# Choosing experts inside the experts' stage, beside memory products and first tiles, and moving the third layer's memory products to the delta rule

## The chip, the cores and the metric

The kernel runs as one program on one core of a Trainium2 chip. The metric is the device time of one execution, in microseconds (us). The data are float32. Matrix products of fp32r tiles are made from a leading and a trailing part of each number, so that a weight is first split on two engines and then multiplied.

## The reference

256 tokens of width 2048 pass one layer of a first model, then two layers of a second. The first layer mixes (short convolution and a state space), attends to a memory of 256 rows, and ends with 16384 experts. Each of the two layers after it uses a memory of its own model, the same for both.

In short, with eight heads and 128 keys a side (the 16384 experts are the pairs of keys):

```
def first_block(x, mem, ...):
    h = h + concat(rms_norm(conv), rms_norm(s5)) @ w_out
    h = h + mem_cross_attention(rms_norm(h), rms_norm(mem), ...)
    h = h + peer(rms_norm(h), w_q, sub_keys, u_tab, v_tab)
    return rms_norm(h, final_norm_g)

def peer(h, w_q, sub_keys, u_tab, v_tab):
    q = (h @ w_q).reshape(..., PEER_HEADS, 2, PEER_HALF)
    s = einsum("blhsk,hsnk->blhsn", q, sub_keys)
    s1, i1 = top_k(s[..., 0, :], 16); s2, i2 = top_k(s[..., 1, :], 16)
    top_s, pos = top_k(s1[:, None] + s2[None, :], 16)
    idx = i1 * 128 + i2 at pos;  g = softmax(top_s)
    act = gelu(h . u_tab[idx]);  return sum(g * act * v_tab[idx])
```

```
def memory_attention(q, gate, mem, mem_gain, w_kv, q_gain, k_gain):
    mk, mv = split_cols(rms_norm(mem, mem_gain) @ w_kv, [512, 512])
    ...
def gdn_branch(...):    
    q, k = l2_norm(q), l2_norm(k)
    o = gated_delta_chunked(...) forward + the same backward
    return rms_norm(o, out_gain) * silu(gate)
```

`gdn_branch` is in the second layer. The memory's keys and values (`mk`, `mv`) depend on the input alone, so they can be computed at any time before the layer that reads them. There are four such products of 2048 x 512: key and value of the second layer (k2, v2) and of the third (k3, v3).

## The kernel before

The program is a row of stages. A stage owns its buffers and semaphores, runs one block of code for each engine, and ends with a barrier of all engines. When a certain number of semaphores is spent (`MOST_SEMS`), they are cleared between two stages.

Weights come as pieces of 512 KB into a ring of four slots (`WeightRing`), loaded by SyncE in the order of the table `JOBS`, four pieces ahead of their use. A piece is split: ScalarE writes its leading part (L415, in the experts L2509), VectorE subtracts to get the trailing part (L420, in the experts L2593), and TensorE multiplies (L548, L2439). Two halves of a linear are thus worked on by three engines in step. The memory products are an exception: they multiply the piece unsplit (`rest_raw`, L2116).

**The load stage** (`load_inputs`) sends small tables, all of x in one transfer of 2 MB, the first constants and four weight pieces from SyncE, and waits for the first three.

**The experts** are three stages (`experts`). The first is the query's linear. The second, "topk" (`choose_experts`), computes scores on TensorE, and VectorE finds the sixteen best of each head (maxima, their indices, replacement; then the sums; then a decoding of places into two indices by comparison, multiplication and reduction, L2276 to L2291). Beside it `MemoryBeside` makes the four memory products in eight turns on TensorE, with one accumulator of two banks, each product evicted by ScalarE (L2126, L2133) before the next starts; SyncE stores the four results to DRAM. The last softmax step (Exp, L2195) stands behind these evictions on ScalarE. The third stage, "dense" (`dense_experts`), multiplies all 16384 experts. Its up half has 32 tiles of eight pieces. A tile's results lie in banks 0 to 3; ScalarE takes the low half out, VectorE adds the rest (L2601, which frees the banks) and scales it, ScalarE applies the gelu, and GpSimd spills the result to DRAM. During the first sixteen tiles TensorE also lays out the gates of the chosen experts as small one-hot products (L2419) in banks 4 to 7, from tables that VectorE weighs (L2614, L2617); for that the choices are first transposed on TensorE (L2475) and copied by VectorE (L2654). GpSimd stores the gates, and at tile 16 fetches two pieces of 2 MB back with four small ones. The down half has 64 steps, which use all eight banks.

**The delta rule** is in the second layer (`even_layer`): `delta_prepare` (transposes L3062, sums of squares as one-column matmuls L1550, spreading of the norms L1582), then the items, then `head_norm` (sums L800, rows L815) and `gate_by_silu`, two stages, and then the output's linear (L548).

## Time and profile before

| what | value |
|---|---|
| three runs | 4055.44, 4059.89, 4064.39 us |
| median | 4059.89 us |
| profiled execution | 4056.16 us |
| its span | 4054.4 us |
| mean granted TensorE clock | 0.97 of full speed |
| TensorE busy | 3849.8 us (95%) |
| VectorE busy | 2435.8 us (60%) |
| ScalarE busy | 1629.8 us (40%) |
| GpSimd busy | 143.4 us (4%) |

A "hole" below is a stretch in which TensorE has no matmul. A row of a timeline gives the start, the length, the engine, the line and the instruction, how many of them in a row, and in brackets the idle time before it and what ended it. PEq is TensorE's own sequencer. Of the 1.8 us between span and execution nothing is seen. The row of granted clock in the page is in tenths of full speed (2.4 GHz); half of it is the lower level, 1.2 GHz.

### The profile page before, as it was taken

What the parts mean: (1) busy time and instruction counts of PE and PEld (TensorE: products, weight loads), DVE (VectorE), ACT (ScalarE), POOL (GpSimd) and SP (SyncE); (2) the same over time, 40 slices, a digit from 0 to 9 for tenths busy, and PEclk for the clock granted to TensorE, in tenths of its full rate; (3) what the DMA queues carried; (4) which work ended last, traced back from release to release, by engine and by line L of the source; (5) the groups of instructions that cost most, each with busy time, mean ns of one, the idle gap of its engine ahead of it and who ended that gap; (6) DMA issues with size and microseconds to landing.
All of it is one profiled execution on the core that took longest, in us unless ns stands there. A gap on an engine that the chain in (4) does not pass through costs nothing. (4 is left out here: it accounts for less than half of the span.)

```text
span 4054.4 us, 66104 instructions
## 1 busy us (share of the span) xinstructions
PE 3849.8 (95%) x25800; PEld 3428.8 (85%) x25800; DVE 2435.8 (60%) x3651; ACT 1629.8 (40%) x2127; POOL 143.4 (4%) x228
## 2 busy tenths in 40 slices
PE   8989899989899999999999999899999889998999
PEld 8975599987688888888888888798999879898989
DVE  5679755459577764556656555544595654565454
ACT  4214344341244444444444444433344333443443
POOL 0002000000000000000000000000000000000000
PEclk9999999999999999999999999899998989998999
DMA  6544355443566676667777776466343015543345
GB/s 221 155 145 140 95 167 167 125 151 111 185 224 222 216 237 231 202 207 240 242 236 238 240 236 206 133 184 206 94 130 110 2 35 174 164 135 125 116 125 166
DMA packets 189107, 682.88 MB, mean 168 GB/s; under 512 B 26568, under 2 KB 29128, under 8 KB 186704
## 3 DMA queue, kind: packets, MB, share of 16 engines
q1 hardware_dynamic: 172624, 608.84, 48.8%
q0 software_dynamic: 16096, 70.26, 4.6%
q8 instruction: 167, 2.74, 0.3%
q10 hardware_dynamic: 160, 0.54, 0.0%
q14 instruction: 60, 0.49, 0.0%
HBM read 639.70 MB, written 39.86 MB: 168 GB/s over the span
## 5 line engine op out<-in xcount | busy, mean ns | idle before, releaser
L2593 DVE TENSOR_TENSOR dense_weights_trailing<-weight_ring,dense_weights_leading 128x1024 fp32r<-128x1024 f32 x512 | 627.2, 1225 | 562.9 <-ACT dense_weights_leading L2509 562.5
L2509 ACT ACTIVATE dense_weights_leading<-weight_ring 128x1024 fp32r<-128x1024 f32 x512 | 542.4, 1060 | 768.7 <-PE dense_banks L2439 368.1
L420 DVE TENSOR_TENSOR held_trailing<-weight_ring,held_leading 128x1024 fp32r<-128x1024 f32 x440 | 537.2, 1226 | 489.1 <-ACT held_leading L415 486.4
L415 ACT ACTIVATE held_leading<-weight_ring 128x1024 fp32r<-128x1024 f32 x440 | 464.6, 1058 | 781.9 <-PE lin_in_acc L548 247.8
L2439 PE MATMUL dense_banks<-pe_parts,dense_weights_leading 128*128 128x512 f32 x2048 | 735.8, 404 | 10.9 <-DVE dense_act_in L2601 9.0
L2468 PE MATMUL dense_banks<-dense_weights_leading,dense_act_parts 128*128 128x512 f32 x2048 | 630.5, 389 | 0.0
L2439 PE MATMUL dense_banks<-pe_parts,dense_weights_trailing 128*128 128x256 f32 x2048 | 554.0, 281 | 0.0
L2439 PEld LDWEIGHTS dense_banks<-pe_parts,dense_weights_leading 128*128 128x128 f32 x2048 | 380.0, 189 | 93.5 <-DVE dense_weights_trailing L2593 9.5
L2468 PEld LDWEIGHTS dense_banks<-dense_weights_leading,dense_act_parts 128*128 128x128 f32 x2048 | 384.4, 188 | 79.8
L2468 PE MATMUL dense_banks<-dense_weights_trailing,dense_act_parts 128*128 128x512 f32 x1024 | 398.3, 389 | 0.0
L2439 PEld LDWEIGHTS dense_banks<-pe_parts,dense_weights_trailing 128*128 128x128 f32 x2048 | 388.5, 190 | 10.0
L548 PE MATMUL lin_out_acc<-lin_out_parts,held_leading 128*128 128x256 f32 x1280 | 233.7, 286 | 15.3 <-DVE held_trailing L420 9.5
L2468 PEld LDWEIGHTS dense_banks<-dense_weights_trailing,dense_act_parts 128*128 128x128 f32 x1024 | 192.2, 188 | 39.9
L548 PEld LDWEIGHTS lin_out_acc<-lin_out_parts,held_leading 128*128 128x128 f32 x1280 | 202.3, 194 | 15.6 <-issue 15.6
L548 PE MATMUL lin_in_acc<-od_parts,held_leading 128*128 128x256 f32 x1024 | 199.8, 296 | 3.2 <-DVE od_parts L660 3.2
L548 PE MATMUL lin_att_acc<-ev_parts,held_leading 128*128 128x256 f32 x1024 | 188.5, 287 | 14.5 <-DVE held_trailing L420 14.5
L548 PE MATMUL lin_in_acc<-ev_parts,held_leading 128*128 128x256 f32 x1024 | 195.4, 292 | 2.0 <-DVEq L646 2.0
L548 PE MATMUL lin_out_acc<-lin_out_parts,held_trailing 128*128 128x256 f32 x640 | 182.5, 285 | 0.0
L548 PEld LDWEIGHTS lin_att_acc<-ev_parts,held_leading 128*128 128x128 f32 x1024 | 162.0, 194 | 16.2 <-issue 15.7
L548 PEld LDWEIGHTS lin_in_acc<-od_parts,held_leading 128*128 128x128 f32 x1024 | 166.8, 198 | 5.9 <-issue 3.4
L548 PEld LDWEIGHTS lin_in_acc<-ev_parts,held_leading 128*128 128x128 f32 x1024 | 163.6, 195 | 4.8 <-DVEq L646 2.4
L548 PE MATMUL lin_in_acc<-lin_in_parts,lin_in_weights_leading 128*128 128x256 f32 x768 | 143.7, 289 | 14.4 <-DVE lin_in_weights_trailing L420 14.4
(735 smaller groups left out, 6871.4 us busy)
## 6 DMA issues: line engine op xcount, KB each, us to landing
weight_ring<-in_w_up SPq DMA_DIRECT2D x256, 512.0 KB, 4.2
weight_ring<-in_w_down SPq DMA_DIRECT2D x256, 512.0 KB, 4.3
weight_ring<-in_w_in SPq DMA_DIRECT2D x176, 512.0 KB, 3.7
weight_ring<-in_w_out SPq DMA_DIRECT2D x112, 512.0 KB, 4.0
weight_ring<-in_w_att SPq DMA_DIRECT2D x64, 512.0 KB, 3.6
weight_ring<-in_w_gate SPq DMA_DIRECT2D x40, 512.0 KB, 3.6
weight_ring<-in_w_key SPq DMA_DIRECT2D x32, 512.0 KB, 3.5
weight_ring<-in_w_value SPq DMA_DIRECT2D x32, 512.0 KB, 3.6
```

The costliest lines, as they stand in the source:

```text
L415: self.nc.scalar.activation(leading, x, ACT.Copy).then_inc(self.led, 1)
L420: return self.nc.vector.tensor_tensor(trailing, x, leading.bitcast(F32), ALU.subtract)
L548: mm = nc.tensor.matmul(acc[:, half, sub], still, moving, start=begin and m == 0, stop=end and m == 2, skip_group_check=not tokens)
L2439: mm = nc.tensor.matmul(to, still, moving, start=begin and m == 0, stop=end and m == 1)
L2468: mm = nc.tensor.matmul(banks[:, down_at[n] + t], still, moving, start=begins and j == 0 and m == 0, stop=ends and j == blocks - 1 and m == 2)
L2509: nc.scalar.activation(ring.leading[:, b], ring.ring[:, b], ACT.Copy).then_inc(split_led, 1)
L2593: v.tensor_tensor(ring.trailing[:, b], ring.ring[:, b], ring.leading[:, b].bitcast(F32), ALU.subtract).then_inc(ring.split, 1)
```

## The change

The change has six parts.

1. The stage "topk" goes away. `dense_experts` starts with scores and the memory products of the second layer (k2, v2); each has two banks of its own. VectorE's work is cut into 110 turns (a generator, `ChooseExperts.on_vector`): 62 before the first tile, then one after each weight piece of tiles 0 to 7 but the third of each, behind which the add of the tile before stands. Pieces are split as before.
2. The gates are laid out in tiles 8 to 23 (`lay_from`, `lay_to`) instead of 0 to 15. From tile 24 odd tiles use banks 4 to 7. GpSimd fetches the first gate piece at tile 24 and the second at tile 28 (`stagger`). ScalarE's Exp stands at the 45th piece of the tiles.
3. To have room, x is kept in DRAM during the experts (`x_kept`, two stores with the fetches of the query's linear, fetched back at the start of the down half); its place holds squares and results of the memory products.
4. k3 is made in `delta_prepare`, v3 in the new `close_delta`, which also takes the place of `head_norm` and `gate_by_silu`. ScalarE multiplies the memory by the layer's gain in the first; GpSimd stores the result for the second, and k3; `close_delta` stores v3 from ScalarE. The table of jobs follows.
5. The load stage sends x in four parts, each followed by a weight piece, and the first linear waits for each part (`src_here`); the stage waits for the small tables alone.
6. `MOST_SEMS` is 72 instead of 60. By the order of the stages semaphores are now cleared at five stage ends instead of three.

```diff
 JOBS = [
-    ("peer_q", 2, 8), ("memk2", 1, 8), ("memv2", 1, 8), ("memk3", 1, 8), ("memv3", 1, 8), ("up", 32, 8), ("down", 32, 8),
-    ("att2", 8, 8), ("dv2", 2, 8), ("in2", 8, 8), ("out2", 4, 10), ("in3", 8, 8), ("upk", 2, 2), ("upv", 2, 2),
+    ("peer_q", 2, 8), ("memk2", 1, 8), ("memv2", 1, 8), ("up", 32, 8), ("down", 32, 8),
+    ("att2", 8, 8), ("dv2", 2, 8), ("in2", 8, 8), ("memk3", 1, 8), ("memv3", 1, 8), ("out2", 4, 10), ("in3", 8, 8), ("upk", 2, 2), ("upv", 2, 2),
...
-    MOST_SEMS = 60
+    MOST_SEMS = 72
...
                 sp.dma_start(k.cols[:], a["cols"]).then_inc(here, 16)
-                sp.dma_start(k.x[:], a["x_t"]).then_inc(here, 16)
+                part(0)
+                ring.load(sp, 0, 0)
                 sp.dma_start(k.consts[:, 0:FIRST_CONSTS], a["consts"][:, 0:FIRST_CONSTS]).then_inc(here, 16)
-                ring.start(sp, 0)
-                sp.wait_ge(here, 48)
+                for n in range(1, X_PARTS):
+                    part(n)
+                    ring.load(sp, 0, n)
+                sp.wait_ge(here, 32)
...
+    lay_from, lay_to, exp_piece, stagger = 8, 24, 44, 4
...
+        def up_banks(i, m):
+            return 4 if from_tile(i, m, lay_to) and m % 2 else 0
...
+                    if t == lay_to:
+                        for b in range(2):
+                            pool.wait_ge(stored[b], 16 * ((lay_to - lay_from) // 2))
+                        fetch_gate(0)
...
+                    if t == lay_to + stagger:
+                        fetch_gate(1)
...
+                for turn in range(memory.JOBS * memory.HALVES):
...
+                    memory.on_tensor(pe, turn)
+                for m in range(lay_from):
+                    up_tile(0, m, False, False)
+                pe.wait_ge(choice.picked, 1)
+                pe.wait_ge(memory.evicted, 2)
...
+                        if c == 2 and not at_tile(i, m, 0):
+                            add(i, m - 1)
+                        if choosing and (c != 2 or m == 0):
+                            next(turns, None)
...
+                for _ in range(choice.EARLY):
+                    next(turns, None)
+                for m in range(lay_from):
+                    up_tile(0, m, False, True)
+                for _ in turns:
+                    pass
                 for n, x in enumerate((first_t, second_t, weight_t)):
                     dve.wait_ge(flipped, n + 1)
...
+            def _(pool):
+                for q in range(4):
+                    pool.wait_ge(featured[q], 16)
+                    pool.dma_start(k.memory_feats[:, quarter(q)], feats[:, quarter(q)]).then_inc(kept, 16)
+                pool.wait_ge(keyed, 1)
+                pool.dma_start(k.memory[2], key[:].rearrange("p a t -> p (a t)")).then_inc(kept, 16)
+                pool.wait_ge(kept, 80)
...
                     norms.sum(pe, 2 * m + 1)
-                for g in order:
+                memory.on_tensor(pe, 0)
+                memory.on_tensor(pe, 1)
+                for at, g in enumerate(order):
                     norms.spread_out(pe, g)
...
+                    if at % 2 == 0 and at < 6:
+                        memory.on_tensor(pe, 2 + at // 2)
+                for c in range(5, 8):
+                    memory.on_tensor(pe, c)
...
                 for g in range(8):
                     norms.square(act, g)
+                    if g >= 4:
+                        q = g - 4
+                        act.wait_ge(mem_here[q], 16)
+                        for c in range(4 * q, 4 * q + 4):
+                            nc.scalar.activation(feats[:, c], feats[:, c], ACT.Copy,
+                                                 scale=k.col("od_mem_norm")[:, c:c + 1]).then_inc(featured[q], 4)
...
+def close_delta(k, ring, y, gate, gain, x_back):
...
+            @block.tensor
+            def _(pe):
+                memory.on_tensor(pe, 0)
+                for c in range(chunks):
+                    if c % 2 == 0:
+                        pe.wait_ge(squared, c // 2 + 1)
...
+                mm.then_inc(summed, 1)
+                memory.on_tensor(pe, 1)
+                pe.wait_ge(inverted, 1)
...
+                for c in range(2, 8):
+                    memory.on_tensor(pe, c)
...
-        head_norm(k, y[:, 0:8], 8, 1, P, k.col("ev_gdn_norm"), here=x_back)
-        gate_by_silu(k, y[:, 0:8], proj[:, 24:32], 8)
+        close_delta(k, ring, y[:, 0:8], proj[:, 24:32], k.col("ev_gdn_norm"), x_back)
```

TensorE at the start of the experts' tiles, before. `one_h` and `pe_mem` are the memory times the gain of the second and of the third layer:

```order
L2205 MATMUL topk_score<-topk_keys,pe_query 128x128 x4
L2116 MATMUL topk_mem_acc<-one_h,weight_ring 128x256 x64
L2116 MATMUL topk_mem_acc<-weight_ring,one_h 128x512 x32
L2116 MATMUL topk_mem_acc<-pe_mem,weight_ring 128x256 x64
L2116 MATMUL topk_mem_acc<-weight_ring,pe_mem 128x512 x32
L2168 UNCONDITIONAL_BRANCH
L2408 UNCONDITIONAL_BRANCH
L2475 MATMUL dense_banks<-consts,pe_first 128x128 x2
L2475 MATMUL dense_banks<-consts,pe_second 128x128 x2
L2475 MATMUL dense_banks<-consts,pe_weight 128x128 x2
L2439 MATMUL dense_banks<-pe_parts,dense_weights_leading 128x512
```

The same place after:

```order
L2182 MATMUL dense_banks<-dense_low,pe_query 128x128 x4
L2117 MATMUL dense_banks<-one_h,weight_ring 128x256 x64
L2117 MATMUL dense_banks<-weight_ring,one_h 128x512 x32
L2453 MATMUL dense_banks<-pe_parts,dense_weights_leading 128x512
L2453 MATMUL dense_banks<-pe_parts,dense_weights_trailing 128x256
```

Two products, the end of a stage and the six transposes no longer stand between the scores and the first tile; the transposes (now L2505) stand behind tile 7.

VectorE where the choices are copied, before, at the head of the first tile:

```order
L2654 COPY dense_first_t<-dense_banks 128x256
L2654 COPY dense_second_t<-dense_banks 128x256
L2654 COPY dense_weight_t<-dense_banks 128x256
L2593 TENSOR_TENSOR dense_weights_trailing<-weight_ring,dense_weights_leading 128x1024
L2614 TENSOR_SCALAR dense_weighed<-consts,dense_second_t,dense_weight_t 128x128 x2
```

After, in tile 8:

```order
L2720 COPY dense_first_t<-dense_banks 128x256
L2720 COPY dense_second_t<-dense_banks 128x256
L2720 COPY dense_weight_t<-dense_banks 128x256
L2641 TENSOR_TENSOR dense_weights_trailing<-weight_ring,dense_weights_leading 128x1024
L2664 TENSOR_SCALAR dense_laying<-consts,dense_second_t,dense_weight_t 128x128 x2
L2641 TENSOR_TENSOR dense_weights_trailing<-weight_ring,dense_weights_leading 128x1024
L2664 TENSOR_SCALAR dense_laying<-consts,dense_second_t,dense_weight_t 128x128 x2
L2641 TENSOR_TENSOR dense_weights_trailing<-weight_ring,dense_weights_leading 128x1024
L2664 TENSOR_SCALAR dense_laying<-consts,dense_second_t,dense_weight_t 128x128 x2
L2650 TENSOR_TENSOR dense_act_in<-dense_low,dense_banks 128x512 x2
```

The add of tile 7 (the last row), which frees its banks, now stands behind three copies, three splits and three weighings; in the first tile there was no earlier tile to add.

TensorE in the preparation of the delta rule, after, from the last sums of squares on. Before, the rows of L1595 (then L1582) stood in one line of x20 behind the sums, and there was no L3121:

```order
L1563 MATMUL prepare_sums<-consts,prepare_sq 128x1 x8
L3121 MATMUL prepare_mem_acc<-prepare_mem_feats,weight_ring 128x256 x16
L1595 MATMUL prepare_rows<-consts,prepare_heads_scale 128x128 x4
L3121 MATMUL prepare_mem_acc<-prepare_mem_feats,weight_ring 128x256 x8
L1595 MATMUL prepare_rows<-consts,prepare_heads_scale 128x128 x8
L3121 MATMUL prepare_mem_acc<-prepare_mem_feats,weight_ring 128x256 x8
...
L3179 MATMUL prepare_turned<-consts,ev_proj 128x128 x4
L3121 MATMUL prepare_mem_acc<-prepare_mem_feats,weight_ring 128x256 x24
```

The first two pieces of the product come between the sums and the rows, three between the rows, and three behind all else.

## Rows read from the trace of the kernel before

**Rows 1.** The page: busy time of the engines; VectorE's splits (line, operation, count, busy, mean).

```profile
PE 3849.8 (95%) x25800; PEld 3428.8 (85%) x25800; DVE 2435.8 (60%) x3651; ACT 1629.8 (40%) x2127; POOL 143.4 (4%) x228
...
L2593 DVE TENSOR_TENSOR dense_weights_trailing<-weight_ring,dense_weights_leading 128x1024 fp32r<-128x1024 f32 x512 | 627.2, 1225 | 562.9 <-ACT dense_weights_leading L2509 562.5
...
L2439 PE MATMUL dense_banks<-pe_parts,dense_weights_leading 128*128 128x512 f32 x2048 | 735.8, 404 | 10.9 <-DVE dense_act_in L2601 9.0
```

**Rows 2.** TensorE's waits: who waited for whom, total us, times, longest.

```profile
PE lin_att_acc L548 <- DVE held_trailing L420: 14.5, 1, 14.5
...
PE dense_banks L2439 <- DVE dense_act_in L2601: 9.0, 15, 5.7
```

**Rows 3.** Groups by line, 900 to 1080 us: busy us, mean ns, idle before.

```profile
L2116 PE MATMUL topk_mem_acc<-one_h,weight_ring 128*128 128x256 f32 x128 | 29.0, 390 | 0.0
...
L2116 PE MATMUL topk_mem_acc<-pe_mem,weight_ring 128*128 128x256 f32 x128 | 27.9, 380 | 1.4 <-ACT mem_v L2133 1.4
...
L2116 PE MATMUL topk_mem_acc<-weight_ring,pe_mem 128*128 128x512 f32 x64 | 27.7, 593 | 1.2 <-ACT mem_k L2126 1.2
```

**Rows 4.** Timeline of VectorE, choosing: last reduce of the first decode; the wait for Exp.

```profile
966.14 2.33 DVE L2291 TENSOR_REDUCE pe_second<-topk_hit_b 128x64 f32<-128x1024 f32 x2
...
1050.42 0.42 DVE L2307 TENSOR_REDUCE topk_total<-topk_raw 128x16 f32<-128x256 f32 x1 [30.26 <-ACT topk_raw L2195]
```

**Rows 5.** Timeline, from the first product to the third weighing of the first tile.

```profile
931.18 28.97 PE L2116 MATMUL topk_mem_acc<-one_h,weight_ring 128*128 128x256 f32 x128
...
1059.86 0.66 PE L2475 MATMUL dense_banks<-consts,pe_first 128*128 128x128 f32 x2 [12.57 <-PEq L2168]
...
1063.26 0.80 PE L2439 MATMUL dense_banks<-pe_parts,dense_weights_leading 128*128 128x512 f32 x1 [1.89 <-DVE dense_weights_trailing L2593]
...
1066.42 0.60 DVE L2614 TENSOR_SCALAR dense_weighed<-consts,dense_second_t,dense_weight_t 128x128 f32<-128x128 f32 x2
```

**Rows 6.** Timeline of TensorE, one-column sums before and in the delta preparation, and its end.

```profile
3066.66 1.84 PE L1550 MATMUL lin_in_beside<-consts,lin_in_biased 128*128 128x1 f32 x16
...
3119.81 3.41 PE L1550 MATMUL prepare_sums<-consts,prepare_sq 128*128 128x1 f32 x16
...
3125.04 6.36 PE L1582 MATMUL prepare_rows<-consts,prepare_heads_scale 128*128 128x128 f32 x40 [1.82 <-DVE prepare_heads_scale L365]
...
3137.52 1.04 PE L3296 MATMUL delta_big<-gd_decay,consts 128*128 128x8 f32 x8 [1.58 <-PEq L3048]
```

**Rows 7.** Timeline of TensorE from the items' end to the output's linear.

```profile
3305.79 6.98 PE L800 MATMUL hnorm_sums<-consts,hnorm_sq 128*128 128x1 f32 x32 [2.30 <-ACT hnorm_sq L789]
...
3314.47 6.13 PE L815 MATMUL hnorm_row<-consts,hnorm_scale 128*128 128x128 f32 x32 [1.70 <-DVE hnorm_scale L365]
...
3330.15 0.77 PE L548 MATMUL lin_out_acc<-lin_out_parts,held_leading 128*128 128x256 f32 x2 [9.55 <-DVE held_trailing L420]
```

**Rows 8.** Windows: stretch, length, busy PE PEld DVE ACT POOL (count), clock, DMA, GB/s.

```profile
1600.00:1650.00 50.00, 49.57 (x279) 42.27 (x277) 26.68 (x27) 22.90 (x26) 1.07 (x2) 1.00 0.64 208
1533.00:1536.00 3.00, 3.00 (x11) 2.52 (x11) 2.37 (x4) 0.04 (x1) 0.00 (x0) 0.50 0.77 303
3107.00:3125.00 18.00, 16.18 (x80) 15.86 (x78) 4.58 (x13) 7.43 (x11) 0.00 (x0) 0.52 0.42 145
```

**Rows 9.** Groups by line, 1250 to 1300 us: VectorE's add of a tile's halves.

```profile
L2601 DVE TENSOR_TENSOR dense_act_in<-dense_low,dense_banks 128x512 f32<-128x512 f32 x4 | 2.7, 684 | 0.9 <-ACT dense_low L2517 0.9
```

**Rows 10.** Timeline of ScalarE, after the gate fetches.

```profile
1525.08 1.06 ACT L2509 ACTIVATE dense_weights_leading<-weight_ring 128x1024 fp32r<-128x1024 f32 x1 [5.45 <-DMA weight_ring<-in_w_up]
```

**Rows 11.** Timeline of the first linear: first matmul; the split that waited for a weight piece.

```profile
14.42 0.77 PE L548 MATMUL lin_in_acc<-lin_in_parts,lin_in_weights_leading 128*128 128x256 f32 x2 [14.42 <-DVE lin_in_weights_trailing L420]
...
23.90 1.06 ACT L415 ACTIVATE lin_in_weights_leading<-weight_ring 128x1024 fp32r<-128x1024 f32 x1 [2.76 <-DMA weight_ring<-in_w_in]
```

**Rows 12.** DMA issues: transfers, KB each, us from issue to landing.

```profile
memory_rows<-mem_v SPq DMA_DIRECT2D x2, 512.0 KB, 4.2
```

More of the change, by code:

```diff
@@ L295, in __init__ @@
         self.x = sb("x", [P, DC, SEQ])
+        self.x_here = [stack.enter_context(nc.semaphore(f"x_here{n}")) for n in range(X_PARTS)]
     def const(self, name):
@@ L2315, in dense_experts, with key_on_scalar, value_on_scalar @@
-def dense_experts(k, ring, parts, scale, first, second, weight, gates, acts, spare):
-    nc = k.nc
-    job = ring.at
-    ring.at += 2
+    def key_on_scalar(self, act):
+        act.wait_ge(self.ring.freed, self.first + 8)
+        self.k.nc.scalar.activation(self.outs[0].rearrange("p (a b) t -> p a (b t)", a=2), self.acc[0],
+                                    ACT.Copy).then_inc(self.evicted, 1)
+    def value_on_scalar(self, act):
+        act.wait_ge(self.ring.freed, self.first + 16)
+        act.wait_ge(self.col_made, 1)
+        value = self.outs[1].rearrange("p (t a) f -> p t (a f)", t=TILES)
+        for t in range(TILES):
+            ins = self.k.nc.scalar.activation(value[:, t], self.acc[1][:, t], ACT.Copy, scale=self.col[:, t:t + 1])
+        ins.then_inc(self.evicted, 1)
@@ L2323, in dense_experts @@
+def dense_experts(k, ring, parts, scale, query, first, second, weight, gates, acts, mem, here, x_kept):
+    nc = k.nc
     groups, per, blocks, slots = 8, 32, ring.BLOCKS, ring.SLOTS
-    assert ring.jobs[job][2:] == ring.jobs[job + 1][2:] == (32, 8)
-    up_base, down_base = ring.first[job], ring.first[job + 1]
-    side, laying_groups, tiles, steps, ahead = 8, 4, 32, 64, 2
-    laying_tiles = 4 * laying_groups
+    side, tiles, steps, ahead = 8, 32, 64, 2
+    lay_from, lay_to, exp_piece, stagger = 8, 24, 44, 4
@@ new lines, in dense_experts @@
+        choice = ChooseExperts(k, s, query, low[:].rearrange("p a b (c f) -> p (a b c) f", f=PEER_KEYS), laying, staging, banks,
+                               first, second, weight, memory)
+        with ExitStack() as early:
+            choice.on_early_memory(lambda n, shape, dt=F32: early.enter_context(nc.sbuf_tensor(f"{s.name}_{n}", shape, dt)))
+        act_parts = s.sb("act_parts", [P, 4, 2, 2, SEQ], F32R)
+        job = ring.at
+        ring.at += 2
+        assert ring.jobs[job][2:] == ring.jobs[job + 1][2:] == (32, 8)
@@ L2437, in up_tile @@
                                 pairs = (rest, high) if end else (high, rest)
-                                for m, (still, moving, to) in enumerate(pairs):
-                                    mm = nc.tensor.matmul(to, still, moving, start=begin and m == 0, stop=end and m == 1)
+                                for n, (still, moving, to) in enumerate(pairs):
+                                    mm = nc.tensor.matmul(to, still, moving, start=begin and n == 0, stop=end and n == 1)
                             if c == 7 and sub == 1:
@@ L3511, in _, with delta_rule @@
                     pass
-def delta_rule(k, proj, ba, spare, out, back):
+def delta_rule(k, ring, proj, ba, spare, out, back):
     nc = k.nc
```

807 lines of the change are left out of this document (467 added, 340 removed).

## The prediction

> **What bounds the kernel now.** I read the page's engine shares first: TensorE is busy 3849.8 us of a 4054.4 us span, VectorE only 60% [rows 1]. So time comes off only where TensorE stops, where it runs at the lower clock, or where its work goes away. I then read TensorE's waits: no total is over 15 us, and the two rows taken here are the largest and the one of the experts' tiles [rows 2]. The idle time lies in some thirty small holes, mostly at stage ends. Last I read the three places that the diff touches.
>
> The experts' start: TensorE does four memory products one after the other, keys 29.0 and 27.9 us, values 27.7 each, with waits of 1.2 to 1.4 us between them [rows 3], while VectorE chooses experts. VectorE is not the bound: after its last reduce at 1020.2 it waits 30.3 us for ScalarE's Exp, which stands behind the last eviction of those products [rows 4]. Then come the end of the stage, 12.6 us of idle TensorE, six transposes, and the first tile's matmul at 1063.26 [rows 5]. The two halves of the third layer's work (about 56 us) delay the experts although nobody there needs them.
>
> The delta preparation: TensorE is the bound, at 1.2 GHz. Sixteen one-column matmuls take 3.41 us there and 1.84 us where the clock is full. There is little idle: 1.8 us before the spreading of the norms into rows, 1.6 us at the end [rows 6]. Closing the delta rule: 26.7 us from the first stop to the output projection's first matmul, with idle pieces of 2.3, 1.7 and 9.55 us and the rest at the low clock (32 one-column matmuls in 6.98 us, 0.22 each, against 1.84/16 = 0.115) [rows 6, 7].
>
> So the change moves 56 us of TensorE work from one place where TensorE is the bound to two where it is almost so. My sum is made against the profiled run's own 4056.16 us; the median of before is 3.7 us above that.
>
> **The change part by part.**
>
> *Start of the tiles.* The products begin at 931.18 [rows 5], as now. Two remain: 29.0 + 27.7, without the 1.2 us wait for an eviction, since they have their own banks. TensorE is at the first tile at 987.9 instead of 1063.26: **-75.4**. After the hole the tile's first matmuls run at the low level (0.80 us for the first [rows 5], 404 ns in the mean [rows 1]), for about 3.2 us by my count; in a continuous stream they don't: **-1.6**. VectorE must be ready: after the first decode, at 968.5 [rows 4], it has one 1.2 us multiplication and seven turns of some 0.95 us, so it is free at 976; the weights' split comes at 983, before 987.9.
>
> *Choosing beside eight tiles.* VectorE's time from 968.5 to 1020.2 is 51.7 us [rows 4]; less the seven turns 45.1, plus 1.3 for the weights of the picks, makes 46.4 us for 48 turns, 0.97 us each. A tile without laying takes 50 x 128/279 = 22.9 us, a piece 2.87 [rows 8]. VectorE has per piece 1.22 for the split [rows 1], four operations of 0.68 us a tile for its eight pieces, 0.34 [rows 9], and 0.97: 2.53: below 2.87, so hidden. Fifty-seven pieces stand before the picks are wanted, for 48 turns, so the picks are ready in the seventh tile. But the decode's turns hold operations like the 2.33 us pairs of reduces [rows 4] or twice as long; four in a row make VectorE some 3 us late, just before an add for which TensorE waits. I take **+2.5** (0 to +8).
>
> *The turn at the ninth tile.* It is laid out at tile 8 now, not at the start. TensorE finishes tile 7, transposes the picks, then needs banks 0 to 3, which VectorE frees by the add that stands behind three copies, three splits and three weighings. In rows: the transposes start at 1059.86 and the third weighing ends at 1067.0 [rows 5], 7.2 us, plus 0.7 for the add [rows 9]: TensorE is held **+7.9**, and after a hole over 5 us it comes back at 1.2 GHz (0.50 at 1533 to 1536, after the 5.7 us hole [rows 2, 8]), about 4 us at half speed: **+2**. What is queued behind is all splits of tile 8.
>
> *Gate fetches.* At tile 16 GpSimd sends two fetches of 2 MB and four smaller; ScalarE then waits 5.45 us for a weight piece, and TensorE 5.7 us [rows 2, 10]. With the low clock after it the stretch loses 8 us. The change sends one fetch at tile 24, the other four tiles later. Bounds 0 and -8; I take **-8**, since the down stage fetches one such piece at a time and TensorE has no wait there. The Trainium skill (DMA: Bandwidth & Descriptors, Queues, rings and completion order) says that each DMA engine takes a packet from each queue in turn; by that the weights would keep half of the rate and no stall could be there, nor be gained. The trace shows the stall, so the measurement decides.
>
> *Two sets of banks in the last eight tiles.* The fifteen waits less the long one are 3.3 us, 0.24 each [rows 2]; with restart 0.2 x 7: **-1.4**.
>
> *x in four parts, x kept in memory.* The first matmul is at 14.42, but the fifth weight piece lands at 23.9 behind 8.4 MB [rows 11], and that order of bytes stays; an earlier start ends in a wait there. Two stores of 1 MB now stand ahead of the query's fifth piece: it lands some 5 us later, at 855, and is needed at 858. Together **+1.5** (-2.5 to +6).
>
> *Key product in the delta preparation.* Eight pieces, 27.9 us. Two stand before the rows, at low clock: +2. They swallow the wait of 1.8 us and make the rows run at full clock (-1.6, half of 3.1 us); ScalarE's sixteen gains of 0.4 us between squares delay the last sums by 0.9. Inside: 27.9 + 2 - 1.8 - 1.6 + 0.9 - 0.5 = 26.9. The end: TensorE now ends 1.6 us before the next stage [rows 6]. Then come VectorE's multiplication 1.3, GpSimd's store 0.6 + 4.2 (nearest row: value rows in 4.2 us [rows 12]), and 1.1 until the next stage's first matmul, out of that 1.6: 7.2, so +5.6. **+32** (25 to 37).
>
> *Value product in the closing.* From the block's start, 3305.1: features land 3.8 later (first piece waits for them, and the sums stand behind it), piece 0 at low clock 5.5, sums 3.6, piece 1 3.5, rows 3.7 at full clock, six pieces 20.8: 3346. Eviction 1.5, store 0.5 + 4.2, then what is left of the 9.55 us hole [rows 7] once its multiplications are gone, 5.1 (of it 1.4 for clearing semaphores): 3357 instead of 3330.15, **+26.5** (22 to 31). That SiLU and its product have left the path is in it.
>
> *Clearing of semaphores.* It takes place at five stage ends instead of three; by the difference between stage ends that have it and those that have not, I estimate it at 1.4 us. One is counted above; the other **+1.5**.
>
> **Sum**: -75.4 - 1.6 + 2.5 + 7.9 + 2 - 8 - 1.4 + 1.5 + 32 + 26.5 + 1.5 = **-12.5 us**, 4043.7 against the profiled run, 4047 against the median.
>
> **The rivals.**
> (a) *The moved products cost less.* The stages at the delta rule run below full speed, 0.52 in much of the preparation [rows 8]. If wide matmuls keep the clock up through sums, transposes and the first items, and stores land in 3.4 us, both terms sit at their lower bounds, 25 and 22: -12.5 - 11.5 = -24, so 4032 to 4036. Against it: sums stay first in the queue.
> (b) *The fetch stalls all the same.* One fetch of 2 MB with four pieces and a spill is still 3.5 of 5.5 MB. With the whole 8 us back: -4.5, time 4039.5 + 12 = 4055, no change to be measured.
> (c) *VectorE becomes the pace while choosing* (slower). It has 0.35 us to spare in 2.87. Every turn's self-waits, and splits that queue behind it, count double if they add over 0.35 us a piece; at 0.8 us more (3.3 a piece) 56 pieces cost 25 us: -12.5 + 25 = +12.5, 4072. For it: its operations are short and each waits for the one before. Against: these waits are inside the 51.7 us already.
> (d) *It doesn't do what it says*: picks late at tile 8, TensorE waiting for VectorE. Nine places are to spare, so this needs (c) first.
>
> **How the numbers follow.** A measurement of this kernel can tell about 0.2%, 8 us, from no change. Forecast 0.50 (4034 to 4052), (a) 0.18, (b) 0.17, (c) with (d) 0.15. Faster by over 8 us: most of the forecast (0.44 of 0.50) and (a): 0.62. Same: 0.06 of the forecast, (b) less 0.01 and 0.01 of (c): 0.23. Slower: 0.15. The range must leave out 0.2: from 4030, the low end of (a), to 4065, in (c)'s lower half.
>
> **What would show it.** Right: first tile's matmul near 988; no TensorE wait for VectorE's split in tiles 0 to 7 over 1 us; one hole of 6 to 7 us after the second group of transposes, near 1172; no hole near the gate fetch; preparation 62 to 64 us long instead of 30.8; closing 52 to 55 instead of 26.7. Wrong: holes in tiles 0 to 7 (c), a hole near the fetch (b), TensorE idle at the ends of the two delta stages over 8 us, or products of over 29 us there.

## The result

| | median | runs | lowest to highest | ratio to before (95%) |
|---|---|---|---|---|
| before | 4059.35 us | 19 | 4053.74 to 4066.65 | |
| changed | 4066.23 us | 19 | 4062.12 to 4073.86 | 1.0018 (1.0011 to 1.0024) |

The change costs 7 us where I had forecast a gain of 12.5. By the bound of the prediction (0.2%) that is no change; the interval leaves out 1. The time lies 1 us above the top of my range. The two profiled executions differ by more than the medians, 10.1 us against 6.9, since the one of before (4056.16 us) is 3.2 us faster than its median; the account below is of these two.

The page of the changed kernel, first lines, answers [rows 1]:

```profile
span 4064.5 us, 65912 instructions
...
PE 3867.5 (95%) x25800; PEld 3426.1 (84%) x25800; DVE 2436.2 (60%) x3653; ACT 1628.2 (40%) x2129; POOL 152.4 (4%) x239
```

TensorE has the same 25800 matmuls as before and is busy 17.7 us longer. So the loss isn't idle time: some matmuls take longer. The page's costliest groups say which. Before, then changed (line, operation, count, busy us, mean ns of one):

```profile
L2468 PE MATMUL dense_banks<-dense_weights_leading,dense_act_parts 128*128 128x512 f32 x2048 | 630.5, 389 | 0.0
```

```profile
L2481 PE MATMUL dense_banks<-dense_weights_leading,dense_act_parts 128*128 128x512 f32 x2048 | 644.0, 396 | 0.0
```

This is the down half of the experts. The diff leaves its arithmetic alone. A window deep inside it counts matmuls: stretch, length, then busy us and count of PE, PEld, DVE, ACT, POOL, then granted clock, DMA share, GB/s; before, then changed:

```profile
2000.00:2400.00 400.00, 400.00 (x1766) 331.21 (x1765) 237.58 (x220) 175.72 (x185) 22.14 (x42) 1.00 0.76 243
```

```profile
2000.00:2400.00 400.00, 400.00 (x1716) 322.03 (x1715) 231.69 (x216) 169.94 (x179) 21.44 (x40) 1.00 0.70 232
```

At full clock and without a hole, 1766 matmuls in 400 us are one every 226.5 ns, 1716 one every 233.1. From start to start the trace of before gives 226.7 ns over all 3072 matmuls of the half, and that of the change 233.3, steadily, after 234.0 in the first eighth. 6.7 ns times 3072 is 20.6 us. The half took 696.5 us before and 717.2 now.

Where the rest went, by the same events in the two traces:

| stretch | before | changed | forecast's term | measured |
|---|---|---|---|---|
| first matmul of tile 0 | 1063.26 | 987.13 | -75.4 | -76.1 |
| end of the up half | 1857.6 | 1788.2 | -74.0 with all its terms | -69.4 |
| length of the down half | 696.5 | 717.2 | none | +20.7 |
| end of the down half to first transposes of the delta preparation | 552.8 | 550.0 | part of +1.5 | -2.8 |
| preparation: first transposes to the items | 30.8 | 61.0 | +32 | +30.2 |
| items | 166.0 | 167.0 | none | +1.0 |
| closing: items' end to the output's first matmul | 26.7 | 57.15 | +26.5 | +30.5 |
| from there to the end | 724.3 | 724.2 | part of +1.5 | 0 |

The right column sums to +10.2 for the rows from the up half's end down, and the spans differ by 10.1. Two of these rows hold for the one profiled execution more than for the kernel. The closing takes 57.15 us in it, but 53.5 to 53.7 in eight of the nine other traces of this closing code (e1, e3 to e7, e11, e14) and 52.0 in e15. And the stretch from the down half to the preparation takes 550.0 us in it, but 551.8 to 554.9 in all eleven others of the changed kernel.

The rows of the changed kernel that answer [rows 5], all from TensorE's timeline: the first matmul of tile 0, then the first matmul of tile 6 (with the hole at the end of tile 5), of tile 8 (with the hole behind the transposes) and of tile 16:

```profile
987.13 0.79 PE L2453 MATMUL dense_banks<-pe_parts,dense_weights_leading 128*128 128x512 f32 x1
...
1129.10 0.77 PE L2453 MATMUL dense_banks<-pe_parts,dense_weights_leading 128*128 128x512 f32 x1 [3.75 <-DVE dense_act_in L2650]
...
1184.49 0.77 PE L2453 MATMUL dense_banks<-pe_parts,dense_weights_leading 128*128 128x512 f32 x1 [6.50 <-DVE dense_act_in L2650]
...
1395.59 0.50 PE L2453 MATMUL dense_banks<-pe_parts,dense_weights_leading 128*128 128x512 f32 x1 [1.92 <-DVE dense_act_in L2650]
```

The closing, which answers [rows 7]:

```profile
3289.40 6.77 PE L3121 MATMUL hnorm_mem_acc<-weight_ring,hnorm_mem_feats 128*128 128x512 f32 x8 [6.23 <-DMA hnorm_mem_feats<-memory_feats]
3296.00 4.07 PE L3712 MATMUL hnorm_sums<-consts,hnorm_sq 128*128 128x1 f32 x32
3299.94 6.61 PE L3121 MATMUL hnorm_mem_acc<-weight_ring,hnorm_mem_feats 128*128 128x512 f32 x8
3306.38 3.73 PE L3720 MATMUL hnorm_row<-consts,hnorm_scale 128*128 128x128 f32 x32
3309.95 20.77 PE L3121 MATMUL hnorm_mem_acc<-weight_ring,hnorm_mem_feats 128*128 128x512 f32 x48
3340.31 0.77 PE L559 MATMUL lin_out_acc<-lin_out_parts,held_leading 128*128 128x256 f32 x2 [9.59 <-DVE held_trailing L431]
```

The preparation, which answers [rows 6] (from TensorE's timeline: the two pieces ahead of the rows, the last three pieces, the items' first matmul):

```profile
3071.08 10.15 PE L3121 MATMUL prepare_mem_acc<-prepare_mem_feats,weight_ring 128*128 128x256 f32 x32
...
3100.42 10.53 PE L3121 MATMUL prepare_mem_acc<-prepare_mem_feats,weight_ring 128*128 128x256 f32 x48
3116.17 1.85 PE L3429 MATMUL delta_big<-gd_decay,consts 128*128 128x8 f32 x8 [5.22 <-PEq L3152]
```

### The profile page after: what moved, and what is told of

Read it like the earlier page. It is cut to its first block and busy times, and to the rows that moved or that the text cites. A ratio compares the mean times of both kernels' runs of the same rounds, so it can differ in the third digit from the quotient of the medians.

```text
span 4064.5 us, 65912 instructions
## 1 busy us (share of the span) xinstructions
PE 3867.5 (95%) x25800; PEld 3426.1 (84%) x25800; DVE 2436.2 (60%) x3653; ACT 1628.2 (40%) x2129; POOL 152.4 (4%) x239
## 5 line engine op out<-in xcount | busy, mean ns | idle before, releaser
L2481 PE MATMUL dense_banks<-dense_weights_leading,dense_act_parts 128*128 128x512 f32 x2048 | 644.0, 396 | 0.0
L559 PE MATMUL lin_in_acc<-lin_in_parts,lin_in_weights_leading 128*128 128x256 f32 x768 | 143.2, 289 | 12.2 <-DVE lin_in_weights_trailing L431 12.2
```

The source lines that it names most:

```text
L559: mm = nc.tensor.matmul(acc[:, half, sub], still, moving, start=begin and m == 0, stop=end and m == 2, skip_group_check=not tokens)
L2481: mm = nc.tensor.matmul(banks[:, 2 * n + t], still, moving, start=begins and j == 0 and m == 0, stop=ends and j == blocks - 1 and m == 2)
```

## Why does a matmul that nobody touched take longer?

In the down half a step has four weight pieces. The stationary operand is `act_parts` (the activations' leading and trailing parts), the moving one the split weights. What the change does there: `act_back`, into which GpSimd fetches, now lies in the query's place, and `act_parts` is allocated behind other buffers. The allocator's places, in bytes from the start of a partition: `act_parts` 173024 before and 178432 now; the split weights 212960 (leading) and 196576 (trailing) in both. The order of the accumulator banks changed too; I made no run for it, but the table at the end of this section has both paces with either order.

Theories at the start: **A**, the place of `act_parts`; **B**, the rhythm in which TensorE enters the half (in single tiles of the up half, in both kernels, a piece takes either 2.77 or 2.83 us, as if one stream had two rhythms); **C**, the new DMA traffic. The first runs:

**e1_after_moved_96.** The changed kernel with 96 bytes ahead of `act_parts`.

```diff
+        s.sb("pad", [P, 24])
         act_parts = s.sb("act_parts", [P, 4, 2, 2, SEQ], F32R)
```

> The changed kernel with 96 bytes of padding ahead of the buffer of the activations' parts (act_parts), nothing else. In the down half a matmul of the changed kernel starts every 233.3 ns, before every 226.7 ns (64 steps, 3072 matmuls: 696.5 us before, 717.2 us after). Theory A, the buffer's place: before it begins 96 bytes behind a multiple of 128 in its partition, as the weights' buffers do, in the change at a multiple of 128. By it the interval falls to 226.7 ns, the down half to 697 us, and the kernel to 0.9966 of the kernel before (-13.5 us). Theory B, the rhythm in which TensorE enters the half: the interval stays at 233.3 ns and the kernel at 1.0018. Theory C, other traffic (fetched pieces now land in the query's place): also no difference, 1.0018.

Measured: 4065.56 us, 1.0018 (1.0008 to 1.0027), no gain; but the interval is 232.4 ns instead of 233.3, and in all of the half:

```profile
2000.00:2400.00 400.00, 400.00 (x1723) 324.28 (x1722) 231.94 (x215) 171.09 (x180) 21.45 (x40) 1.00 0.69 233
```

Theory A in the form "as many bytes behind a multiple of 128 as the weights" is refuted. Yet a shift of 96 bytes changed the interval a little.

**e2_before_moved_32.** The kernel before with 32 bytes of padding between `act_back` and `act_parts`.

```diff
-        act_back, act_parts = s.sb("act_back", [P, 4, 2, SEQ]), s.sb("act_parts", [P, 4, 2, 2, SEQ], F32R)
+        act_back, _, act_parts = s.sb("act_back", [P, 4, 2, SEQ]), s.sb("pad", [P, 8]), s.sb("act_parts", [P, 4, 2, 2, SEQ], F32R)
```

> The kernel before with 32 bytes of padding ahead of act_parts, so that it begins at a multiple of 128 bytes, as in the changed kernel, and nothing else. Theory A (place): the interval of matmuls in the down half rises from 226.7 to 233.3 ns, the half from 696.5 to 717 us, the kernel to 1.0050 of before. Theories B (rhythm at entry) and C (traffic): no difference, 1.0000 and 226.7 ns.

Measured: 4077.79 us, 1.0048 (1.0031 to 1.0064). Thirty-two bytes cost the kernel before 19 us, and its down half has exactly the pace of the changed kernel:

```profile
2000.00:2400.00 400.00, 400.00 (x1716) 322.08 (x1715) 230.78 (x214) 169.85 (x178) 21.97 (x41) 1.00 0.74 237
```

None of the change's traffic is in this kernel, so theory C can't be what slows it.

**e3_after_hole_at_down.** TensorE enters the half after a wait.

```diff
-                            pe.wait_ge(added, 2 * (tiles - 1) + max(0, n - 1))
+                            pe.wait_ge(added, 2 * tiles)
```

> The changed kernel, where TensorE waits at the first matmul of the down half until the last tile of the up half is added (a hole of some 3 us), so that it doesn't run on in the rhythm of the up half. Theory B (rhythm at entry): the interval falls from 233.3 to 226.7 ns, the down half is shorter by 20 us, the kernel by about 17. Theory A (place of act_parts): 233.3 ns stays, the kernel is some 3 us longer.

Measured (one run): 4069.61 us, a hole of 1.41 us at the entry, and 233.3 ns as in the changed kernel. Theory B is refuted: another entry, the same pace.

So the place decides, but by which rule? Both places that are slow, 173056 and 178432, are multiples of 256, and e1's place, 178528, is 96 behind one. The fast place, 173024, is 224 behind one, and so are both buffers of split weights. Theory **A2**: the place modulo 256, 512 or 1024, tested in the changed kernel by three paddings (`[P, 184]`, `[P, 56]`, `[P, 120]` instead of `[P, 24]` in the diff of e1).

**e5_after_moved_736.**

> Places of act_parts in a partition so far: 173024 (before: 226.7 ns between matmuls of the down half), 173056 (233.3), 178432 (the change: 233.4), 178528 (232.7). The split weights begin at 212960 and 196576. Here the changed kernel with 736 bytes ahead of act_parts, which then begins at 179168, 6144 bytes behind its place before, so that it has the place of before in every period up to 2048 bytes. Theory A2, the place within such a period (the same as that of the weights modulo 1024): 226.7 ns, the down half 697 us, the kernel 0.9966 of before (4045 us). Theory D, that 32 bytes more slow the kernel before by something else, and the change is slow by its other traffic (fetches into the query's place): 233 ns, 1.0018.

Measured: 4049.86 us, 0.9978 (0.9968 to 0.9988), the down half 700.9 us. Against the changed kernel's 1.0018 that is 0.40%, 16.2 us, and the half alone is 16.3 us shorter. The pace is that of before:

```profile
2000.00:2400.00 400.00, 400.00 (x1766) 331.24 (x1765) 238.14 (x221) 175.04 (x184) 22.05 (x41) 1.00 0.72 238
```

The half is still 4.4 us longer than before, and that is at its beginning. From 1790 to 1830 us this run has 161 matmuls, a hole of 2.5 us and a clock of 0.96, while the changed kernel has 172 and no hole. The hole ends with VectorE's split of a weight piece. x is fetched back there (2 MB); whether that makes the piece late wasn't tried.

```profile
1790.00:1830.00 40.00, 37.52 (x161) 30.66 (x160) 23.34 (x25) 17.22 (x20) 4.80 (x9) 0.96 0.78 273
```

**e6_after_moved_224 and e7_after_moved_480.**

> As the run before, with 224 bytes: act_parts begins at 178656, like its place before modulo 256 and 512, but not modulo 1024. Theory A2 with a period of 256 or 512 bytes: 226.7 ns. With a period of 1024 or more: 232 to 233 ns. Theory D: 233 ns.

> As the run before, with 480 bytes: act_parts begins at 178912, like its place before modulo 256 alone. Theory A2 with a period of 256 bytes: 226.7 ns; with 512 or more: 232 to 233 ns. Theory D: 233 ns.

Measured: 4046.06 and 4040.51 us (one run each), both 226.7 ns, the half 698.5 and 698.0 us. Theory D is refuted. The period is 256 bytes: 512 or more would make e6 or e7 slow, and by 128 or less 96 (e1) and 224 would be the same place.

**e10_before_moved_256.** The control: the kernel before, with `[P, 64]` in the diff of e2.

> The kernel before with 256 bytes of padding ahead of act_parts, a control to the run with 32 bytes. Theory A2 (place modulo 256): 226.7 ns and the time of before. If any shift slows the kernel before (theory D): 233.3 ns and +20 us.

Measured: 226.7 ns and a down half of 696.5 us, as before. The time, 4063.51 us in one run, is within the runs of before; the trace is already 7 us late at tile 0 (1070.4), ahead of anything that the padding touches.

**e9_before_both_moved.** Is it `act_parts` alone, or the two operands together? In the kernel before, `act_parts` as in e2, and the split weights moved from 224 to 0.

```diff
+        s.stack.enter_context(nc.sbuf_tensor(f"{s.name}_right_pad", [P, 56], F32, side="right"))
         ring.split_slots(s)
```

> So far 226.7 ns between the down half's matmuls wherever act_parts begins at 224 modulo 256 bytes (173024, 178656, 178912, 179168), 232.3 to 232.7 at 96 (178528), 233.3 at 0 (173056, 178432). The split weights begin at 224 modulo 256 in all of these. Here the kernel before with act_parts at 0 (173056) and also the split weights moved by 224 bytes, to 0 (212736 and 196352). Theory R, that stationary and moving operand must begin at the same place modulo 256: 226.7 ns, the kernel as before, but the up half, where the moving operand (pe_parts) stays at 224, slower. Theory S, that the place of act_parts alone decides: 233.3 ns, kernel +20 us. Theory M, that each operand has its own cost when it isn't at 224: more than 233.3 ns.

Measured: 4054.49 us (one run), 226.7 ns. Theories S and M are refuted. What I had expected of theory R for the up half did not come: it isn't slower there. That leaves, for the down half, R (same place) and W (weights at 0 are fast anyway). Three more runs:

**e13_before_weights_0.** The padding of e9 without that of e2.

> The kernel before with the split weights moved to 0 modulo 256 bytes (212736 and 196352) and act_parts where it was, at 224. Theory R (stationary and moving operand begin at the same place modulo 256): 232 to 234 ns between the down half's matmuls instead of 226.7, the kernel some 18 to 20 us longer. Theory W (weights at 0 are fast wherever act_parts begins): 226.7 ns and the time of before.

Measured: 4077.28 us (one run), 233.3 ns:

```profile
2000.00:2400.00 400.00, 400.00 (x1716) 321.28 (x1715) 230.79 (x214) 170.31 (x178) 21.97 (x41) 1.00 0.74 237
```

Here `act_parts` is where it was in the kernel before, and the half is as slow as in the change. W is refuted.

**e14_after_weights_0.** The padding of e9 in the changed kernel.

> The changed kernel with the split weights moved to 0 modulo 256 bytes, where its act_parts is (178432), and act_parts untouched. Theories R and W: 226.7 ns, the down half 697 to 701 us instead of 717, the kernel 0.997 to 0.998 of before instead of 1.0018. If only a move of act_parts helps: 233 ns, 1.0018.

Measured: 4051.50 us, 0.9980 (0.9971 to 0.9990), with no move of `act_parts`. The half takes 703.4 us, 6.9 more than before, all in its first eighth, where a hole of 4.24 us ends with VectorE's split of a weight piece.

**e15_after_both_96.** The padding of e1, and `[P, 32]` on the right side.

> The changed kernel with act_parts at 96 modulo 256 bytes (178528, where 232.7 ns were measured with the weights at 224) and the split weights moved to 96 as well. Theory R: 226.7 ns. If only the places 0 and 224 are fast: 232 to 233 ns.

Measured: 4047.25 us (one run), 226.7 ns.

All of it in one table. Places are modulo 256, the counts are from the window 2000 to 2400:

| kernel | act_parts | split weights | matmuls in 400 us | start to start |
|---|---|---|---|---|
| before | 224 | 224 | 1766 | 226.7 ns |
| e5, e6, e7 (changed) | 224 | 224 | 1766 | 226.7 |
| e10 (before) | 224 | 224 | 1766 | 226.7 |
| e9 (before) | 0 | 0 | 1767 | 226.7 |
| e14 (changed) | 0 | 0 | 1766 | 226.7 |
| e15 (changed) | 96 | 96 | 1767 | 226.7 |
| changed, e3 | 0 | 224 | 1716 | 233.3 to 233.4 |
| e2 (before) | 0 | 224 | 1716 | 233.3 |
| e13 (before) | 224 | 0 | 1716 | 233.3 |
| e1 (changed) | 96 | 224 | 1723 | 232.4 |

The eight kernels of the table whose operands begin at the same place modulo 256 have one pace, the five with different places are 2.5 to 3% slower, in both kernels, with either operand moved and with either order of the banks. Three pairs of different places were tried (0 with 224, 224 with 0, 96 with 224). That is shown for this half: fp32r, stationary operand `act_parts`, moving operand 512 columns of split weights. It isn't shown elsewhere. In the up half the roles are others (weights stationary, `pe_parts` at 224 moving), and there e13, with the weights at 0, isn't slower: 1004 matmuls from 1660 to 1840 us (1008 in e9), where before has 1000. What in the chip makes the difference was not tried and stays open.

## The other terms

**e4_after_add_first.** The turn at tile 8.

```diff
                 for _ in turns:
                     pass
+                add(0, lay_from - 1)
                 for n, x in enumerate((first_t, second_t, weight_t)):
```

> The changed kernel with VectorE's add of tile 7 ahead of the three copies of the picks instead of behind three splits and three weighings of tile 8. Forecast's step: TensorE's hole behind the transposes (6.50 us at 1178) comes from the add that frees banks 0 to 3; it falls to about 1 us, and the low clock after it goes (piece 0 of tile 8 takes 5.19 us instead of 2.8): 7.5 us less in tiles 7 and 8. Rival: the copies and the first weighings hold TensorE anyway (through the laying matmuls from piece 4 on), then less than 3 us come back.

Measured (one run): 4060.85 us. The hole goes from 6.50 to 4.21 us and has another releaser, VectorE's first split of tile 8, which now stands behind add, scaling and copies:

```profile
1178.57 0.79 PE L2453 MATMUL dense_banks<-pe_parts,dense_weights_leading 128*128 128x512 f32 x1 [4.21 <-DVE dense_weights_trailing L2641]
```

Tile 7 with the transposes takes 27.7 us instead of 29.6, tile 8 26.8 in both: the clock falls after a hole of 4.21 us as well (0.50 from 1178.6 to 1183.8 us). So 2 us came back, within what the rival said (less than 3), though TensorE is now held by that first split and not through the laying matmuls. The add was what held the banks, as I had said; my size for the cure was wrong.

**e11_after_both_fetches.** `stagger` 0 instead of 4.

> The changed kernel with both fetches of 2 MB at tile 24 (stagger 0 instead of 4). Forecast's step (one fetch at a time doesn't stall the weights, worth 8 us): TensorE has a hole of 5 to 6 us in tile 25 or 26 and one piece at the low clock behind it, the kernel is 7 to 8 us longer. Rival (the other bank set or the later place hides the fetches): no hole over 1 us, the same time.

Measured (one run): 4067.39 us; no hole of TensorE over 0.3 us from tile 23 to the end of the up half. After the fetches the DMA engines are as full as they were before (1.00, 403 GB/s), and TensorE runs on:

```profile
1640.00:1660.00 20.00, 20.00 (x115) 17.39 (x114) 8.98 (x10) 6.39 (x7) 0.00 (x0) 1.00 1.00 403
```

ScalarE's longest wait for a weight piece is 2.6 us there, 5.45 before [rows 10]:

```profile
ACT dense_weights_leading L2536 <- DMA weight_ring<-in_w_up: 5.0, 3, 2.6
```

The 8 us were won, but not by the stagger: the rival is right. Between the two are a later tile, another order (the second gate piece now goes behind the four small ones), and two bank sets. Which of them shortens the wait wasn't tried.

**e8_close_sums_first.** In the closing, the sums ahead of piece 0.

```diff
-                memory.on_tensor(pe, 0)
                 for c in range(chunks):
...
                 mm.then_inc(summed, 1)
+                memory.on_tensor(pe, 0)
                 memory.on_tensor(pe, 1)
```

> The changed kernel, where in the closing of the delta rule the 32 one-column sums stand ahead of the first weight piece of the value product instead of behind it (TensorE waited 6.23 us for the fetched features there). Forecast's step (features land late and the sums stand behind them): sums start 2.3 us after the items' end and take 7.0 us at the low clock, then piece 0 at the low clock 6.6; output's first matmul some 4 us earlier, 53 us behind the items' end instead of 57.15. Rival (clock eats it): pieces 0 and 1 and the sums all at the low clock, less than 1.5 us won.

Measured (one run): 4061.19 us; 51.6 us from the items' end to the output's first matmul instead of 57.15:

```profile
3287.02 6.99 PE L3711 MATMUL hnorm_sums<-consts,hnorm_sq 128*128 128x1 f32 x32 [2.30 <-ACT hnorm_sq L3691]
3293.86 8.75 PE L3121 MATMUL hnorm_mem_acc<-weight_ring,hnorm_mem_feats 128*128 128x512 f32 x16
```

The wait of 6.23 us is gone, and pieces 0 and 1 together take 8.75 us instead of 6.77 + 6.61: the clock falls once and not twice. Against the profiled execution of the changed kernel that is 5.5 us, more than I expected. But in the other traces with the closing unchanged it takes 53.5 to 53.7 us (52.0 in one), so the edit is worth about 2 us, nearer to the rival than to my step.

**e12_best.** The changed kernel with 480 bytes ahead of `act_parts`, the edits of e4 and e8, and `EARLY = 65` instead of 62, for the hole of 3.75 us at the end of tile 5. VectorE's timeline of the changed kernel has four multiplications of 2.3 us between 1108.6 and 1122.7 us, with splits between them. The last two are shown; two reductions of 1.21 us and three more splits follow, and then the add, at 1128.27.

```profile
1117.07 2.28 DVE L2258 TENSOR_TENSOR dense_staging<-dense_staging,dense_wheref 128x2048 f32<-128x2048 f32 x1
1119.28 1.22 DVE L2641 TENSOR_TENSOR dense_weights_trailing<-weight_ring,dense_weights_leading 128x1024 fp32r<-128x1024 f32 x1
1120.41 2.28 DVE L2261 TENSOR_TENSOR dense_staging<-dense_staging,dense_wheref 128x2048 f32<-128x2048 f32 x1
```

> The changed kernel with four edits: 480 bytes ahead of act_parts (down half 698 us instead of 717), the add of tile 7 ahead of the copies (-3.9 us by the look at it), sums ahead of the first piece in the closing (-3.9), and 65 turns ahead of tile 0 instead of 62, so that the four multiplications of 2.3 us don't stand together ahead of tile 5's add (hole of 3.75 us and one piece at the low clock, -5). If all four add up: 0.9920 of before (4026 us against 4058), 0.9967 by the first alone.

Measured: 4039.85 us, 0.9951 (0.9937 to 0.9964), 20 us under the kernel before, whose median beside it is 4060.12. It beats both kernels. It isn't the 0.9920 for which I hoped (the four steps of that expectation add up to 4032 us, not to its 4026). Its trace has the down half at 699.4 us; tiles 4 to 6 at 71.2 us instead of 75.2, with a hole of 2.16 left; the closing at 51.7. Most of what is missing is in the first step: the padding alone, timed in e5, gave 0.9978 where I had counted on 0.9967. From there to 0.9951 are about 11 us, close to the 12.8 expected of the other three edits. But one run with the padding alone (e7, 4040.51 us) was as fast as e12, and the three edits were not timed one by one, so their worth isn't shown.

## Why the prediction was wrong, point by point

- **The missing term.** The sum went over what the diff adds, removes and moves on the engines' queues. It had no term for the down half, since no instruction there changes. The change does move the buffers, and that was 20.7 of the 22.6 us between forecast (-12.5) and trace (+10.1). So the step that failed is the assumption that the down half costs nothing since its instructions stay as they are; what it cost is 6.7 ns in each of 3072 matmuls, because `act_parts` moved from 224 to 0 modulo 256 bytes while the weights stayed at 224. With the operands at the same place the rest of the sum stands close to what was forecast: e5 and e14, timed, have medians 8.1 and 7.4 us under before, and of what they lack to -12.5, 4.4 and 6.9 us are at the beginning of the down half.
- **Start of the tiles, -75.4:** right, -76.1. VectorE was free at 976 as said and waited 5.58 us for the first weights. **Warm first tile, -1.6:** nearly as said. The granted clock is 1.00 there (0.50 before), and the tile's first piece takes 3.18 us instead of 4.37, -1.2; only the first matmul is as long as before, 0.79 us.
- **Choosing beside tiles, +2.5 (0 to 8):** tiles 0 to 4 take 23.2 us in the mean, as good as hidden, and the picks are ready in tile 6. But four large turns together made a hole of 3.75 us at the end of tile 5 (I had said 3 us late) and then a piece at the low clock (5.26 us instead of 2.8), which I hadn't counted: tiles 5 and 6 are 6.2 us over. +7.5 altogether, at the top of its bounds. Rival (c) didn't occur: its point, 3.3 us of VectorE a piece, wasn't reached, and no wait repeats over the tiles.
- **The turn at tile 8, +9.9:** the mechanism right, its size 6.50 us of hole and 2.4 for piece 0 at the low clock, 8.9.
- **Gate fetches, -8:** the size right: tiles 16 to 18 take 78.6 us before, tiles 24 to 26 69.3 now, and some 1.3 of these 9.3 us are the banks'. The reason is wrong (e11), so the size was luck. Rival (b) is out. The number in it, "4039.5 + 12", doesn't give its 4055; the median less 4.5 does.
- **Two sets of banks, -1.4:** tiles 25 to 31 take 22.6 us each, before 23.0: -3.0.
- **Not foreseen:** at two of the turns of the loop over laying tiles VectorE stands still for 5.62 us (1384 and 1490), which the profile puts to "issue", and TensorE loses 1.92 us each. The two tiles that end there take 28 us instead of 26 in every trace of a changed kernel. In the kernel before no such pause is in the trace. Why was not tried.

```profile
1389.90 1.23 DVE L2641 TENSOR_TENSOR dense_weights_trailing<-weight_ring,dense_weights_leading 128x1024 fp32r<-128x1024 f32 x1 [5.62 <-issue]
```

- **Load and x in memory, +1.5:** the scores start at the same time to 0.1 us in both: nothing. (In seven of the eleven other traces of the changed kernel they start up to 2 us earlier, at 898.4 to 899.4 instead of 900.7.) The first matmul came 2.2 us sooner (waits of 12.2 instead of 14.4) and the gain was gone by the next stages, as said.
- **Preparation, +32:** +30.2, inside its bounds. The idle time at its end is 5.22 us instead of the 7.2 of the sum.
- **Closing, +26.5 (22 to 31):** +30.5 in the profiled execution (my own terms give +27.1, not +26.5). The features came 0.8 us later, and the second piece ran at the low clock, 6.61 us instead of 3.5. In my sum the clock had recovered by then, but behind the one-column sums it is low again: 0.51 in the window of that piece.

```profile
3300.00:3306.00 6.00, 6.00 (x9) 2.48 (x9) 1.12 (x6) 3.69 (x6) 0.00 (x0) 0.51 0.01 4
```

In the other traces with this closing both low stretches are shorter, here in e11; there the term is +26.9 (53.5 against 26.7), as forecast.

```profile
3293.65 5.23 PE L3121 MATMUL hnorm_mem_acc<-weight_ring,hnorm_mem_feats 128*128 128x512 f32 x8 [5.91 <-DMA hnorm_mem_feats<-memory_feats]
3298.71 3.63 PE L3712 MATMUL hnorm_sums<-consts,hnorm_sq 128*128 128x1 f32 x32
3302.20 5.38 PE L3121 MATMUL hnorm_mem_acc<-weight_ring,hnorm_mem_feats 128*128 128x512 f32 x8
```

- **Clearing of semaphores:** 1.2 us more at the attention's linear, 1.8 at the last output, and less where it went away. In the whole stretch nothing of it can be told from the spread of the traces.
- **Rival (a), -24:** with preparation at +30.2 and closing at +26.9 to +30.5 the moved products weren't cheaper. The rule of the Trainium skill that I had weighed (DMA: Bandwidth & Descriptors, Queues, rings and completion order: each engine takes a packet from each queue in turn) doesn't alone say who stalls: the same fetches stall TensorE in the kernel before and don't in e11.

## What to carry to other kernels

A change that allocates buffers in another order can slow matmuls that it doesn't touch: when two traces show the same instructions with another mean duration at the same clock, compare the places of their operands before looking for traffic. Here it paid to let stationary and moving operand begin at the same place modulo 256 bytes, for a few bytes of padding: 16 us, where all the rest of the change gains 8. Work that is hidden behind another engine on average still shows where its largest pieces meet the one operation that the other engine waits for, and such a hole cost twice here, once as a hole and once as the low clock behind it: those of 3.75, 4.21 and 6.50 us did, those of 1.92 us didn't. And before a row of one trace is explained, see the same row in the other traces of the same code: the closing's 3.5 us extra were in one of ten.

## What the runs showed of the hardware that I had not expected

- fp32r matmuls of 512 columns in the down half start every 226.7 ns when stationary and moving operand begin at the same place modulo 256 bytes in their partitions (224, 0 or 96), and every 232.4 to 233.3 ns in the three pairs of different places that were tried. Thirty-two bytes were worth 0.48% of this kernel. The up half showed no such effect.
- A matmul stream can have several steady paces at full clock: in single tiles of the up half a piece takes 2.77 us (tiles 0, 2 and 5 of the changed kernel) or 2.83 us (tiles 1, 3 and 4) with the same operands.
- Two fetches of 2 MB beside the weights stall TensorE for 5.65 us in one place and not at all in another, with the DMA engines full in both (DMA share 1.0).
